# A two-block transformer kernel: modulation rows copied ahead of half the scaling, gates weighted by GpSimd, new recurrent preparation, key selection and sparse attention

## The reference, cut to what matters

```python
shift, scale, gate = split(silu(cond) @ w_ada + b_ada, 3)
x = rms_norm(h, norm_w) * (1 + scale) + shift
# differential attention, layer 0
a = p[:, :, 0] - lam * p[:, :, 1]
o = rms_norm(a @ v, subln_w, 1e-5) * (1.0 - lam_init)
o = o * silu(z)
# recurrent layer (RWKV part)
rw_p = rw_p + (prev - rw_p) * mu          # prev: one token earlier
decay = exp(-exp(w_log)); a = sigmoid(a0 + al @ a2)
kk = heads(k * k_k); kk = kk / max(sqrt(sum(kk * kk)), 1e-12)
k = k * (1.0 + (a - 1.0) * k_a)
bonus = sum(r * k * r_k) * v
# sparse layer
s = relu(einsum('bqhd,bsd->bqhs', qi, ki)); score = einsum('bqh,bqhs->bqs', wi, s)
score = where(key_pos <= q_pos, score, -1e30); _, sel = top_k(score, 64)
pr = softmax(where(valid, q @ k[sel] * 128 ** -0.5, -1e30)); o = pr @ v[sel]
```

## Time and profile before

| what | value |
|---|---|
| median of 3 runs | 2609.46 us (2609.13 to 2609.96) |
| the profiled execution's own time | 2609.79 us |
| its span, first to last instruction | 2608.0 us |
| mean granted clock of TensorE | 0.973 |

### The profile page before, as it was taken

How to read it: one execution, slowest core, us unless ns; L and a number is a source line. 1 busy time by engine, 2 the same in 40 slices (tenths; PEclk the granted TensorE clock), 3 DMA queues, 4 the chain that set the end, 5 groups by cost and what they waited for, 6 DMA issues and landing times. The chain is left out here.

```text
span 2608.0 us, 62512 instructions
## 1 busy us (share of the span) xinstructions
PE 2435.0 (93%) x22898; PEld 2290.2 (88%) x22898; DVE 1729.3 (66%) x3987; ACT 1297.9 (50%) x2351; POOL 597.7 (23%) x490
## 2 busy tenths in 40 slices
PE   5999798897969999999999999969999999999998
PEld 3998566487958999999999999858999999999997
DVE  3032632639554976888999666674976888998665
ACT  3322643355325666555444554545665555444554
POOL 1335133157226950000000000626940000000000
PEclk8999999998989999999999999989999999999999
DMA  8554022043103554444444554314555444444552
GB/s 270 169 165 135 17 73 94 17 124 113 60 17 130 187 189 166 162 166 157 171 166 161 177 192 161 118 45 135 183 192 177 162 161 161 162 161 163 190 190 85
DMA packets 153861, 373.36 MB, mean 143 GB/s; under 512 B 8784, under 2 KB 102880, under 8 KB 137216
## 3 DMA queue, kind: packets, MB, share of 16 engines
q1 hardware_dynamic: 151216, 369.31, 42.1%
q10 hardware_dynamic: 2512, 2.24, 0.3%
HBM read 370.48 MB, written 1.05 MB: 142 GB/s over the span
## 5 line engine op out<-in xcount | busy, mean ns | idle before, releaser
L2744 ACT ACTIVATE w_hi<-ring 128x512 fp32r<-128x512 f32 x1024 | 645.3, 634 | 683.2 <-PE bank L2799 364.0
L2750 DVE TENSOR_TENSOR w_lo<-ring,w_hi 128x512 fp32r<-128x512 f32 x864 | 595.0, 691 | 308.8 <-ACT w_hi L2744 304.0
L2781 PE MATMUL bank<-x_hi,w_hi 128*128 128x256 f32 x2048 | 578.6, 283 | 3.9 <-DVE w_lo L2750 3.7
L2799 PE MATMUL bank<-hidden_hi,w_hi 128*128 128x256 f32 x2048 | 577.6, 282 | 0.0
L2799 PE MATMUL bank<-hidden_hi,w_lo 128*128 128x256 f32 x2048 | 573.1, 280 | 0.0
L2781 PE MATMUL bank<-x_hi,w_lo 128*128 128x256 f32 x2048 | 572.7, 280 | 0.0
L2781 PE MATMUL bank<-x_lo,w_hi 128*128 128x256 f32 x2048 | 571.5, 279 | 0.0
L2799 PE MATMUL bank<-hidden_lo,w_hi 128*128 128x256 f32 x2048 | 570.2, 278 | 0.0
L374 POOL TENSOR_TENSOR w_lo<-ring,w_hi 128x512 fp32r<-128x512 f32 (+2 forms) x264 | 350.5, 1347 | 689.1 <-ACT w_hi L365 682.4
L2781 PEld LDWEIGHTS bank<-x_hi,w_hi 128*128 128x128 f32 x2048 | 385.9, 188 | 4.8 <-ACT hidden L2874 4.0
L2781 PEld LDWEIGHTS bank<-x_lo,w_hi 128*128 128x128 f32 x2048 | 386.0, 188 | 0.0
(11 more groups left out here) (517 smaller groups left out, 4101.2 us busy)
## 6 DMA issues: line engine op xcount, KB each, us to landing
ring<-in_peer_uT SPq DMA_DIRECT2D x128, 1024.0 KB, 4.9
ring<-in_peer_v SPq DMA_DIRECT2D x128, 1024.0 KB, 4.8
ring<-in_even_w_in SPq DMA_DIRECT2D x26, 1024.0 KB, 5.3
ring<-in_ada_w SPq DMA_DIRECT2D x24, 1024.0 KB, 7.9
ring<-in_odd_w_in SPq DMA_DIRECT2D x12, 1024.0 KB, 5.3
ring<-in_even_w_out SPq DMA_DIRECT2D x8, 1024.0 KB, 5.8
ring<-in_odd_w_out SPq DMA_DIRECT2D x8, 1024.0 KB, 5.2
ring<-in_peer_w_q SPq DMA_DIRECT2D x8, 1024.0 KB, 5.2
```

Of the source, the lines that this page charges most:

```text
L2744: act.activation(k.hi[q][:, :], k.ring[slot][:, q * PART:q * PART + PART], ACT.Copy).then_inc(k.hi_ready, 1)
L2750: eng.tensor_tensor(k.lo[q][:, :], k.ring[slot][:, q * PART:q * PART + PART], k.hi[q][:, :].bitcast(F32), ALU.subtract).then_inc(k.lo_read ...
L2781: mm = pe.matmul(k.bank[s][:, j * T:j * T + T], a[q][:, w], b[:, cc, :], start=(cc == 0 and n == 0), stop=(cc == KC - 1 and n == 2))
L2799: mm = pe.matmul(out, a[q][:, w], b[:, j, :], start=first and cc % 2 == 0 and n == 0, stop=last and cc % 2 == 1 and n == 2, skip_group_che ...
```

## The change

In the head VectorE scales four chunks (`SCALED`), copies the rows, and makes the four low parts itself; it scales the other four chunks in the next block. In differential attention GpSimd multiplies the gates by `subln_w` in four operations, VectorE finishes a unit in one operation, and the constant factor goes into the root. In `Preparation` the store of a raw block writes two scaled copies on ScalarE, so that a shift is one addition; constant factors go into the exponentials; ScalarE makes the factor of k2, the square of kk and kk; the squares are summed to eight rows, the reciprocal is taken of 8x256, and a second product ahead of block 9 spreads it. In `KeySelection` Relu works in PSUM, the first accumulation starts from the mask, and two pairs of operations become one or none. `sparse_attention` takes two heads at once and, for the first 128 queries, only the first 128 keys; ScalarE makes the high half of the output. One more constant (`headrow`) is loaded.

```diff
-            for c in range(KC):
+            for c in range(SCALED):
                 rms.scale(dve, c)
             dve.wait_ge(k.mod_summed, FRONT)
             dve.tensor_copy(rows, k.bank[0][:, 0:WB]).then_inc(k.mod_kept, 1)
+            ahead.low(dve)
             dve.wait_ge(k.mod_turned, 1)
             add_bias(k, dve, k.bank[1], 0, FRONT)
             weigh_scale(k, dve, 0)
-
-        @block.gpsimd
-        def _(pool):
-            ahead.low(pool)
...
-            if c < KC and self.early != "scaled":
+            if c < KC and (self.early != "scaled" or c >= SCALED):
                 self.scale(dve, c)
...
-                dve.scalar_tensor_tensor(out=out, in0=k.bank[4 * (u % 2) + 3][:, 0:B_V], scalar=inv[:, u, 0:1], in1=row("subln_w"),
+                z = proj[:, m, 6 * A_W + h * B_V:6 * A_W + h * B_V + B_V]
+                dve.wait_ge(k.pool.sem, weighted[m])
+                dve.scalar_tensor_tensor(out=out, in0=k.bank[4 * (u % 2) + 3][:, 0:B_V], scalar=inv[:, u, 0:1], in1=z,
                                          op0=ALU.mult, op1=ALU.mult).then_inc(finished, 1)
-                dve.wait_ge(finished, u + 1)
-                z = proj[:, m, 6 * A_W + h * B_V:6 * A_W + h * B_V + B_V]
-
-                S.step(dve.scalar_tensor_tensor(out=out, in0=out, scalar=1.0 - (0.8 - 0.6 * math.exp(0.0)), in1=z,
-                                                op0=ALU.mult, op1=ALU.mult))
...
-            k.ask_root(dve, ss[:, :], 1.0 / B_V, 1e-5)
+            dve.wait_ge(finished, n_units)
+            k.ask_root(dve, ss[:, :], 1.0 / B_V / share ** 2, 1e-5 / share ** 2)
...
+        @block.gpsimd
+        def _(pool):
+            for m in range(TC // P):
+                z = proj[:, m, 6 * A_W:6 * A_W + B_H * B_V].rearrange("p (h v) -> p h v", h=B_H)
+                assert k.pool.step(pool.tensor_tensor(z, z, spread(row("subln_w"), 1, B_H), ALU.mult)) == weighted[m]
...
-            return copy(kind, eng, b["raw"][:, 2 * (blk - 2):2 * (blk - 2) + 2, :], both)
+            for f in (2 * blk - 4, 2 * blk - 3):
+                x = bank[:, (f % 2) * T:(f % 2) * T + T]
+                k.act.step(eng.activation(b["raw"][:, f, :], x, ACT.Copy, scale=b["rest"][:, f:f + 1]))
+                last = eng.activation(b["shift"][:, f, :], x, ACT.Copy, scale=k.col("mu_rkv", f))
+                if f % 2 == 0:
+                    k.act.step(last)
+            return last
...
         if blk == 8:
-            pe.wait_ge(self.logs, 1)
             pe.wait_ge(self.norm_sq, 1)
             for f in range(4):
-                mm = pe.matmul(half((7, 2)[f // 2], f), b["headones"], b["t1"][:, f, :], start=True, stop=True)
+                mm = pe.matmul(k.bank[7][0:8, 0:T], b["headsel8"][:, 8 * f:8 * f + 8], b["t1"][:, f, :], start=f == 0, stop=f == 3)
+            mm.then_inc(self.norm_sum, 1)
+        if blk == 9:
+            pe.wait_ge(self.logs, 1)
+            pe.wait_ge(self.norm_inv, 1)
+            for f in range(4):
+                mm = pe.matmul(half((2, 3)[f // 2], f), b["headrow"][0:8, f * P:f * P + P], b["inv8"][0:8, :], start=True, stop=True)
             mm.then_inc(self.norm_sum, 1)
...
+            act.wait_ge(self.shifted, 3)
+            for f in range(4):
+                act.activation(b["shift"][:, f, :], b["a"][:, f, :], ACT.Identity, bias=b["rest"][:, 12 + f:13 + f],
+                               scale=k.col("k_a", f)).then_inc(self.gates, 1)
...
+            act.wait_ge(self.shifted, 4)
+            for f in range(4):
+                ins = act.activation(b["t1"][:, f, :], b["raw"][:, 4 + f, :], ACT.Square, scale=k.col("k_k", f))
...
+            ins.then_inc(self.norm_sq, 1)
+            for f in range(4):
+                ins = act.activation(b["kk"][:, f, :], b["raw"][:, 4 + f, :], ACT.Copy, scale=k.col("k_k", f))
+                if f < 3:
+                    k.act.step(ins)
+            ins.then_inc(self.exps, 1)
+        if blk == 7:
+            k.root(act, b["inv8"][0:8, :])
...
     def shift(self, dve, c0, c1):
-        k, S, x, d = self.k, self.k.dve, self.b["raw"], self.b["shift"]
-        S.step(dve.tensor_tensor(d[:, c0:c1, 1:T], x[:, c0:c1, 0:T - 1], x[:, c0:c1, 1:T], ALU.subtract))
-        S.step(dve.tensor_scalar(d[:, c0:c1, 0:1], x[:, c0:c1, 0:1], -1.0, None, ALU.mult))
-        S.settle(dve)
-        S.step(dve.tensor_tensor(d[:, c0:c1, :], d[:, c0:c1, :], spread(k.col("mu_rkv", c0, c1 - c0), 2, T), ALU.mult))
-        S.settle(dve)
-        S.step(dve.tensor_tensor(x[:, c0:c1, :], x[:, c0:c1, :], d[:, c0:c1, :], ALU.add))
-        S.settle(dve)
+        x, d = self.b["raw"], self.b["shift"]
+        dve.tensor_tensor(x[:, c0:c1, 1:T], x[:, c0:c1, 1:T], d[:, c0:c1, 0:T - 1], ALU.add).then_inc(self.shifted, 1)
+        self.nshifted += 1
+        dve.wait_ge(self.shifted, self.nshifted)
...
-            do(dve.tensor_tensor(A(kk), raw[:, 4:8, :], spread(k.col("k_k", 0, 4), 2, T), ALU.mult))
-            dve.tensor_tensor(A(t1), A(kk), A(kk), ALU.mult).then_inc(self.norm_sq, 1)
         if blk == 6:
-            dve.wait_ge(self.gates, 8)
-            do(dve.tensor_scalar(tmp, A(b["a"]), -1.0, None, ALU.add))
-            do(dve.tensor_tensor(tmp, tmp, spread(k.col("k_a", 0, 4), 2, T), ALU.mult))
-            do(dve.scalar_tensor_tensor(out=A(b["k2"]), in0=tmp, scalar=1.0, in1=raw[:, 4:8, :], op0=ALU.add, op1=ALU.mult))
-            do(dve.tensor_tensor(A(b["rk"]), raw[:, 0:4, :], A(b["k2"]), ALU.mult))
-            S.step(dve.tensor_tensor(A(b["rk"]), A(b["rk"]), spread(k.col("r_k", 0, 4), 2, T), ALU.mult))
+            dve.wait_ge(self.gates, 12)
+            do(dve.tensor_tensor(A(b["k2"]), tmp, raw[:, 4:8, :], ALU.mult))
+            S.step(dve.tensor_tensor(A(b["rk"]), raw[:, 0:4, :], A(b["k2"]), ALU.mult))
         if blk == 7:
             self.shift(dve, 8, 12)
+            dve.wait_ge(self.norm_sum, 1)
+            dve.tensor_scalar(b["inv8"][0:8, :], k.bank[7][0:8, 0:T], 1e-24, None, ALU.max).then_inc(k.radicand, 1)
+            k.asked += 1
             dve.wait_ge(self.exps, 3)
             S.step(dve.tensor_tensor(A(b["rt"]), raw[:, 0:4, :], A(b["dec"]), ALU.mult))
+            dve.wait_ge(k.rooted, k.asked)
+            dve.reciprocal(b["inv8"][0:8, :], b["inv8"][0:8, :]).then_inc(self.norm_inv, 1)
             S.step(dve.tensor_tensor(A(b["kt"]), A(b["k2"]), A(b["neg"]), ALU.mult))
...
-            dve.wait_ge(k.rooted, k.asked)
-            do(dve.reciprocal(A(t1), A(t1)))
-            do(dve.tensor_tensor(A(kk), A(kk), A(t1), ALU.mult))
+        if blk == 9:
+            dve.wait_ge(self.exps, 7)
...
+            for f in (0, 2):
+                S.step(dve.tensor_tensor(kk[:, f:f + 2, :], kk[:, f:f + 2, :], pair((2, 3)[f // 2]), ALU.mult))
...
-        if blk == 9:
-            dve.wait_ge(self.exps, 6)
...
-                pe.wait_ge(self.rectified, h - 3)
+                pe.wait_ge(self.used, 2 * (h - 3))
                 self.score(pe, h)
...
         act.wait_ge(self.scored, h + 1)
-        if h >= 3:
-            act.wait_ge(self.used, 2 * (h - 2))
-        act.activation(self.relu[:, h % 3, :, :], self.bank(h)[:, :].rearrange("p (m t) -> p m t", m=2), ACT.Relu).then_inc(self.rectified, 1)
+        act.activation(self.bank(h)[:, :], self.bank(h)[:, :], ACT.Relu).then_inc(self.rectified, 1)
...
             dve.wait_ge(self.rectified, h + 1)
-            r, w = self.relu[:, h % 3, m, :], self.b["wi"][:, m, h:h + 1]
-            if h == 0:
-                dve.tensor_scalar(score[:, m, :], r, w, None, ALU.mult).then_inc(self.used, 1)
-            else:
+            r, w = self.bank(h)[:, m * T:m * T + T], self.b["wi"][:, m, h:h + 1]
+            if h:
                 dve.wait_ge(self.used, n - 1)
-                dve.scalar_tensor_tensor(out=score[:, m, :], in0=r, scalar=w, in1=score[:, m, :],
-                                         op0=ALU.mult, op1=ALU.add).then_inc(self.used, 1)
+            before = score[:, m, :] if h else self.const("notcausal")[:, m, :]
+            dve.scalar_tensor_tensor(out=score[:, m, :], in0=r, scalar=w, in1=before, op0=ALU.mult, op1=ALU.add).then_inc(self.used, 1)
...
-        S.step(dve.tensor_tensor(score[:, :, :], score[:, :, :], const("causal"), ALU.mult))
-        S.settle(dve)
-        S.step(dve.tensor_tensor(score[:, :, :], score[:, :, :], const("notcausal"), ALU.add))
-        S.settle(dve)
...
-        S.step(dve.tensor_scalar(bias[:, :, :], score[:, :, :], 10 * NEG, None, ALU.is_lt))
-        S.settle(dve)
-        S.step(dve.tensor_tensor(bias[:, :, :], bias[:, :, :], const("causal"), ALU.mult))
+        S.step(dve.scalar_tensor_tensor(out=bias[:, :, :], in0=score[:, :, :], scalar=10 * NEG, in1=const("causal"), op0=ALU.is_lt, op1=ALU.mult))
...
+def sparse_attention(k, b, mixT):
+
+
+    nc = k.nc
+    pairs = [(m, h) for m in range(2) for h in range(0, S_H, 2)]
...
+    keys = lambda u: P * (pairs[u][0] + 1)
+    scores = lambda u: k.bank[(0, 1, 6, 7)[u % 4]]
```

(80 more changed lines are left out.)

103 lines of the change are left out of this document (59 added, 44 removed).

## The result

The changed kernel takes 2580.74 us, the median of four runs (2575.37 to 2584.53), against 2609.71 for the kernel before on the same chip: a ratio of 0.9887, 95% interval 0.9869 to 0.9905. The forecast was 2577.0, range 2564 to 2590. The profiled execution took 2580.63. Two executions, one of the kernel before at 4004.72 us and one of an experiment at 6277.83, had a granted clock of 0.56 and 0.45 and stand in no ratio.

A forecast was written before the change was run, and what follows sets the result against it. TensorE was busy 93% of the span, so savings were sought at its gaps and each touched stage's last release. Five terms, 5.0 + 3.6 + 9.7 + 5.0 + 9.5 = 32.8, off 2609.8 gave 2577.0 us, range 2564 to 2590.

The forecast's parts named there:

- B: Differential attention: one VectorE operation fewer per unit's finish, 0.32 us a unit; 3.6 us saved, bounds 2.3 to 5.1.
- C: Recurrent projection with Preparation: 16.3 us of waits and low clock within reach, less 6.6 of new costs; 9.7 saved.
- D: KeySelection: cheaper accumulations from PSUM and fewer mask operations, less GpSimd contention; 5.0 us saved, bounds 3 and 7.
- E: Sparse attention: heads in pairs, narrow ones 1.95 and wide ones 2.65 us apart; 9.5 saved, bounds 4 and 12.
- A: Head (modulation): four chunks scaled instead of eight, so the block ends near 44.7 for 49.7; 5.0 us saved, bounds 2 to 7.
- The lower bound (chunks without cover): Head: the four chunks moved to the next block would cost 2.5 us if not hidden between other work there.
- may slow a VectorE operation or two by 0.2: Differential attention: cost allowed for GpSimd's four weightings running beside VectorE while the pipeline fills, 0.2 us.
- 4.1 of low clock: Recurrent projection: time TensorE loses at lowered clock after two waits, 2.0 and 2.1 us, counted as within reach.
- my first rival: Recurrent projection: ScalarE, given 10.3 us more work, takes the stall over; saving there about 0, total 2587; chance 0.16.
- The 0.755 each: KeySelection: old price of each of eight accumulations, 6.04 us in all, from SBUF with GpSimd working.
- the 0.8 taken off for the low clock: Sparse attention: 0.8 us deducted from the 10.3 saving because the first pairs run at TensorE's low clock.
- The rival of a low clock in this stage: Sparse attention: at half clock TensorE becomes the bound, four wide pairs cost 2.0 us more each; total 2585; chance 0.11.

The follow-up runs named there:

- run 6: Changed kernel with GpSimd's four subln_w weightings moved one block ahead, into the turning of q and k: 2576.26 us, ratio 0.9880 against the kernel before.
- run 11: Changed kernel with weightings one block earlier and block 5's four Preparation gates on VectorE behind the shift: 2576.07 us, ratio 0.9878 against the kernel before.
- run 10: Changed kernel with the four gate operations of Preparation's block 5 on VectorE, ahead of the shift: 2582.45 us, ratio 0.9894 against the kernel before.
- part_prep: Kernel before with the new Preparation alone (its stores, constant tiles and bonus included): 2600.46 us, ratio 0.9966.
- run 7: Changed kernel with each of GpSimd's four weightings cut into four of 128x128, same place: 2577.59 us, ratio 0.9878 against the kernel before.
- run 9: Changed kernel with all 256 keys for the first 128 queries of sparse attention, still in pairs: 2582.12 us, ratio 0.9902 against the kernel before.

## Why the prediction was right, and which terms were not

With 14 traces each stage has a median for either code (five traces with the code before, six to nine with the code after; kernels that edit the stage further are left out):

| stage | before | after | saved | predicted |
|---|---|---|---|---|
| start to even projection | 54.1 | 49.0 | 5.2 | 5.0 |
| differential attention | 51.2 | 49.2 | 1.9 | 3.6 |
| recurrent projection | 108.3 | 100.4 | 7.9 | 9.7 |
| KeySelection's stage | 47.8 | 43.9 | 4.0 | 5.0 |
| sparse attention | 36.9 | 25.4 | 11.5 | 9.5 |
| all other stages | | | -0.4 | 0 |

Before rounding the sum is 29.9 against the 32.8 predicted, and 26.3 to 29.5 by the two measurements of the whole. The choice of places was right: each touched stage pays, and in four of the five the whole time shows it too. The forecast's own sizes were less good than its nearness: B, C and D were too large by 4.5 and E too small by 2.0, and that E covers part of the others is luck.

*A* held step by step: the copy at 40.35 for "near 41", the block's end at 43.55 for 44.7, of which 0.6 is the earlier start. The lower bound (chunks without cover) didn't come about. One trace more or less would move this term: with the old head the even projection starts at 52.5 to 55.0 in five traces, with the new one at 48.5 to 49.7 in nine.

*B* is the term that failed most: 1.9 for 3.6. The removed step is right, 0.33 a unit for 0.32 (2.30 to 1.97). I had weighed the rule of the Trainium skill ("VectorE: DVE Perf Modes", section "The DRAIN you can't avoid") that the semaphore between two operations costs nothing, by which 0.21 a unit would have been saved; the loop decides for the dropped wait's own price of about 0.1. What failed is "may slow a VectorE operation or two by 0.2": one operation of 0.17 lost 1.1, at the head of the pipeline, where all waited for it. Runs 6 and 11, without it, get 0.7 to 1.5 back; the rest of the 1.7, some 0.2 to 1.0, stays open. I had a row with GpSimd stretching VectorE in hand (1.67 for 0.69, in D) and used it there, but in B asked only how long GpSimd takes, and not which short operation it would hold.

*C* came out at 9.5 between the two profiled executions, 7.9 by the medians; the profiled one of before had this stage 1.6 longer than four others with the same code. Inside the term two errors work against each other. The waits fell by more than I said, by 9.2 for 8.2: 15.5 to 6.3, with the new one before block 7 at 2.96 for the 2.8 predicted, and none before block 9, where I had 1.2 (it is there, 1.1, in runs 10 and 11). And the "4.1 of low clock" was not to be had: TensorE's busy time went from 93.3 to 92.9 in the two profiled executions, and by medians from 91.7 to 91.2. In the trace of after three stretches at a lowered clock still lose 4.8. Part of that trades places with the waits: there block 6 ran at 0.77 and TensorE waited 2.96 behind it; in part_prep it ran at 1.00 and waited 4.5, and the stage was as long. Part of it does cost time: in runs 6 and 7, with this stage unchanged and the same waits before blocks 6 and 7, the third stretch (617.50 to 627.50 above, at 0.86) ran at full clock and the stage took 98.7. Here that stretch in run 6:

```profile
610.87:620.87 10.00, 9.85 (x77) 9.16 (x76) 5.61 (x5) 4.48 (x9) 9.66 (x6) 1.00 0.32 105
```

ScalarE as the new limit was my first rival; it did take part, but not the whole gain: run 11 takes 97.1, against 98.7 in run 6, which differs in this stage by the gates alone, and 100.4 by the median, so 1.6 to 3.3. The operation that remains of the shift cost 1.22, 1.21 and 1.50 and not 2.19: the row of before had GpSimd in it.

*D*: 4.0 for 5.0, inside the bounds, and 4.4 between the profiled executions. 2.8 for the accumulations (predicted 3.1), 3.4 for the masks, 2.3 of contention for 2.0. The mechanism held: PSUM makes the operation not shorter (0.48 both ways, alone) but free of GpSimd. The 0.755 each was a mean of operations of 0.48 and of up to 1.52, not a price beside GpSimd.

*E*: 11.4 for 9.5, near the upper bound. Seven steps from first to last reciprocal were forecast at 16.5 and took 16.3, but not for the reason given: the narrow steps were 2.4, 1.6 and 3.5, not 1.95. The first norming came 4.5 after the start and not 5.7, because TensorE's first products are half as wide (with the full width in run 9 it came 5.9 after), and the 0.8 taken off for the low clock was already in those steps. The rival of a low clock in this stage fell: the narrow pairs did run at 0.50 to 0.72, with stages of 25.2 to 26.0, and the wide ones at 1.00.

By the medians B and C were 3.5 too large and D 1.0, E 2.0 too small. In the profiled pair the touched stages gave 33.1 and the whole 29.2; the 4 between has no cause in the change. The trace of before was short in the second attention where 13 others agree, and it was long in the touched stages, by 0.9 to 1.6 each in the first three. What follows sparse attention, the output projection and the second expert layer, varied from 861.1 to 866.5 with the same code. What decides, from one execution to the next, where the low stretches fall stays open.

## What to carry to other kernels

Before work goes to GpSimd, list VectorE's operations that read and write SBUF in the time when it will run, the tiniest first, and ask what waits behind each: it can stand as long as GpSimd's running operation. Put such work beside reads of PSUM, or cut it in pieces. Take no stage's time from one trace: here 4 us of seeming loss were a property of the one trace of the kernel before. And an engine that is moved off the path still ends its block.

## What the runs showed of the hardware

- A TENSOR_SCALAR of 128x2 took 0.17 alone, 1.26 beside GpSimd's operations of 1.23, and 0.48 beside pieces of 0.44. The same operation of 128x1 kept its 0.15 beside GpSimd. Reductions and copies from PSUM (1.29 for two, 0.69) and the choice's MAX8 (0.62 for two) and MATCH_REPLACE8 (0.28 and 0.41) kept their times beside GpSimd.
- A TENSOR_TENSOR of 128x1024 took 1.20 to 1.23 with GpSimd idle and mostly 2.06 to 2.32 beside it, though a few took 1.15 to 1.89.
- With gaps in TensorE's first 5 us of sparse attention its granted clock was 0.50 to 0.72 in the next 6; with none, 0.95. Half the columns for half the queries were worth 1.2 us of 26.7.
- An untouched stage of the second attention had a granted clock of 0.82 in six traces (37.1 to 37.3 us), 0.87 in seven (36.4 to 36.9) and 0.89 in one (34.7). One kernel's times, four to twelve executions run together, spread over 4 to 10 us.
